# FFN 2's up projection by Strassen's algorithm, F in two groups, and two weight sums by an accumulating DMA

## The chip, the cores and the metric

The kernel runs on 1 core of one Trainium2 chip. The metric is the device time of the whole program in microseconds (us); smaller is better. Times are given for three runs, and a profile shows one further execution with every instruction's start and duration.

## The reference

One layer of a decoder trunk, in float32, for 512 tokens of width 1024. A vector c gives nine modulation vectors (shift, scale and gate for three sub-layers). Around a mixer stand two half-step SwiGLU FFNs:

```python
h = modulate(rms_norm(x, norm_ffn2_g[l]), mod[:, 2, 0], mod[:, 2, 1])
x = x + HALF_STEP * mod[:, 2, 2][:, None, :] * swiglu(h, ffn2_w_in[l], ffn2_w_out[l])
```

where `swiglu(h, w_in, w_out)` splits `h @ w_in` into g and u and gives `(silu(g) * u) @ w_out`. Here h is 512 x 1024, `w_in` 1024 x 5632 (2816 columns of g, 2816 of u) and `w_out` 2816 x 1024. A final RMSNorm over x is the output.

## The kernel before, in words

Activations lie transposed, features over the 128 partitions and the T = 512 tokens along the free axis. D = 1024 is KD = 8 blocks of 128, F = 2816 is KF = 22 blocks. TensorE (PE) multiplies in float32r. Each factor is split into a high part (rounded to float32r) and a rest, and a product is three matmuls into the same PSUM bank: high x high, high weight x rest, rest weight x high (`product`, L1136 to L1138). Each matmul is preceded by a load of its 128 x 128 weight tile.

The stages follow one another: modulation and FFN 1, mixer, the norm ahead of FFN 2, FFN 2 up, FFN 2 down, final norm. In FFN 2's **up projection** one tile is one block of F: `pair` runs 8 blocks of K x 2 (gate and up) x 3 terms = 48 matmuls of 512 columns into two PSUM banks. The first of the 22 tiles is done in halves of 256 tokens, as the norm hands them over. In the **down projection** one block is one of the 8 blocks of D: 22 x 3 = 66 matmuls, in two chunks of 11 x 3. The last block is done in two halves of 256 tokens. In the second FFN, PE also transposes the block before (L1253) for the output.

Each engine runs its own program in order, and semaphores tie them. SyncE (SP) loads raw weights, double-buffered: `load_pair` (L300) 1.05 MB a tile in two DMAs, as soon as the slot's raw weights have been split (`lo_ready`). ScalarE (ACT) casts a slot to its high part (`split_hi`, L497), does silu (L552), and casts the product (L560). VectorE (DVE) subtracts for the rest (`split_lo`, L706), multiplies silu(g) with u (L824), and subtracts for the product's rest (L837). In the down projection DVE adds a block to x (L854), scales it for the output, and adds up squares (L865). GpSimd (POOL) is nearly idle there; it splits three weight slots elsewhere (L429), one of them beside the norm ahead of FFN 2. The norm itself runs in steps of 256 tokens: DVE scales (L752), ACT adds the shift and rounds (`h_his`, L504), DVE takes the rest (L759).

## Time and profile before

| | |
|---|---|
| Three runs | 931.53, 932.56, 933.40 us (median 932.56) |
| Span of the profiled execution, first to last instruction | 929.1 us |
| Median of the runs over that span | 3.5 us |
| PE busy | 885.1 us (95%), 4155 matmuls |
| DVE, ACT, POOL busy | 495.9, 266.4, 60.3 us |
| DMA | 123.64 MB, 133 GB/s over the span |
| Mean granted clock of TensorE | 0.977 of full speed |

The profiled execution's own device time is not listed apart from its span; the runs' median stands 3.5 us over it. A busy share is an average over stages, so what one stage is worth is read from that stage. Matmuls are pipelined, and their durations in the trace overlap the next one, so the distance between two starts is what one costs.

### The profile page before, as it was taken

The page shows a single profiled execution, that of the slowest core. Times are in us where ns is not written, and L with a number is a line of the kernel's source. Part 1 is how long each engine was busy: PE and PEld are TensorE (multiplying, and loading weights), DVE is VectorE, ACT ScalarE, POOL GpSimd, SP SyncE. Part 2 cuts the span into 40 slices and gives each one's busy share as a digit, 9 for nine tenths or more (in the row PEclk, how much of TensorE's full clock was granted, in tenths as well). Part 3 has the DMA queues.
Part 4 walks back from the last instruction along what each step waited for, and adds up shares of the span by engine and source line. Part 5 has one row for each costly group of instructions (what it writes and reads, how often), then busy time and mean ns, then how long its engine had stood idle before and what let it go on. Part 6 is the DMA issues. An engine that isn't in the chain of part 4 may idle for free.

```text
span 929.1 us, 11471 instructions
## 1 busy us (share of the span) xinstructions
PE 885.1 (95%) x4155; PEld 735.3 (79%) x4155; DVE 495.9 (53%) x734; ACT 266.4 (29%) x306; POOL 60.3 (6%) x49
## 2 busy tenths in 40 slices
PE   4499999999999999998999989999999999999997
PEld 3387888888888888896887878888888888888886
DVE  3899877777775656547635574333333333233332
ACT  5123222322222222224324243222223322222222
POOL 2810000000000000002340030000000000000000
PEclk9599999999999999999999999999999999999998
DMA  9929766666646565444332313333333332333322
GB/s 275 294 70 256 203 194 194 198 195 199 183 136 194 153 191 148 130 136 124 83 111 69 91 47 90 92 103 108 104 91 90 90 90 64 91 94 94 93 63 91
DMA packets 205381, 123.64 MB, mean 133 GB/s; under 512 B 4280, under 2 KB 203052, under 8 KB 205356
## 3 DMA queue, kind: packets, MB, share of 16 engines
q1 hardware_dynamic: 205356, 123.28, 46.8%
q8 instruction: 18, 0.29, 0.1%
q14 instruction: 7, 0.06, 0.0%
HBM read 121.17 MB, written 2.10 MB: 133 GB/s over the span
## 4 chain that ended last, share of the span: by engine, by line
PE 91%; DVE 4%; SPq 1%; DMA 1%; issue 1%; ACT 1%; POOL 0%; DVEq 0%
PE ps L1136 29%; PE ps L1138 29%; PE ps L1137 29%; DVE acc_first L962 2%; DVE h_lo L759 1%; PE ps L1378 1%; DMA ada_first<-in_w_ada_dram 1%; PE ps L1379 1%; PE ps L1380 1%; SPq L300 1%; DVE w_lo L717 0%; PE ps L1270 0%; DVE work L752 0%; PE ps L1428 0%; PE ps L1418 0%
## 5 line engine op out<-in xcount | busy, mean ns | idle before, releaser
L1136 PE MATMUL ps<-h_hi,w_hi 128*128 128x512 f32 (+1 forms) x784 | 308.6, 394 | 7.7 <-DVE h_lo L759 6.2
L1138 PE MATMUL ps<-h_hi,w_lo 128*128 128x512 f32 (+1 forms) x784 | 306.3, 391 | 0.0
L1137 PE MATMUL ps<-h_lo,w_hi 128*128 128x512 f32 (+1 forms) x784 | 303.7, 387 | 0.0
L706 DVE TENSOR_TENSOR w_lo<-w_raw,w_hi 128x2048 fp32r<-128x2048 f32 (+1 forms) x81 | 165.2, 2039 | 179.2 <-ACT w_hi L497 179.2
L497 ACT CAST w_hi<-w_raw 128x2048 fp32r<-128x2048 f32 (+1 forms) x83 | 140.7, 1695 | 141.7 <-PE ps L1138 112.4
L1136 PEld LDWEIGHTS ps<-h_hi,w_hi 128*128 128x128 f32 x784 | 149.6, 191 | 37.2 <-DVE h_lo L759 6.8
L1138 PEld LDWEIGHTS ps<-h_hi,w_lo 128*128 128x128 f32 x784 | 149.3, 190 | 32.9
L1137 PEld LDWEIGHTS ps<-h_lo,w_hi 128*128 128x128 f32 x784 | 149.2, 190 | 31.7
L1136 PE MATMUL ps<-a_hi,w_hi 128*128 128x512 f32 (+1 forms) x396 | 146.1, 369 | 0.0
L1138 PE MATMUL ps<-a_hi,w_lo 128*128 128x512 f32 (+1 forms) x396 | 145.6, 368 | 0.0
L1137 PE MATMUL ps<-a_lo,w_hi 128*128 128x512 f32 (+1 forms) x396 | 144.7, 365 | 0.0
L552 ACT ACTIVATE work<-ps 128x512 f32<-128x512 f32 x44 | 26.3, 597 | 327.5 <-PE ps L1138 327.5
L824 DVE TENSOR_TENSOR work<-work,ps 128x512 f32<-128x512 f32 x44 | 30.2, 687 | 161.6 <-ACT work L552 161.5
L802 DVE SCALAR_TENSOR_TENSOR ada_acc<-ada_raw,c_act,ada_acc 128x256 f32<-128x256 f32 x196 | 95.0, 485 | 7.0
L1137 PEld LDWEIGHTS ps<-a_lo,w_hi 128*128 128x128 f32 x396 | 74.4, 188 | 13.0
L1138 PEld LDWEIGHTS ps<-a_hi,w_lo 128*128 128x128 f32 x396 | 74.4, 188 | 12.5
L1136 PEld LDWEIGHTS ps<-a_hi,w_hi 128*128 128x128 f32 x396 | 74.4, 188 | 12.1
L429 POOL TENSOR_TENSOR w_lo<-w_raw,w_hi 128x2048 fp32r<-128x2048 f32 x3 | 13.6, 4540 | 437.3 <-ACT w_hi L520 381.3
L504 ACT ACTIVATE h_hi<-work,mod 128x256 fp32r<-128x256 f32 (+1 forms) x36 | 20.4, 579 | 50.5 <-DVE work L752 50.3
L837 DVE TENSOR_TENSOR a_lo<-work,a_hi 128x512 f32 (+1 forms) x44 | 30.1, 684 | 0.0
L759 DVE SCALAR_TENSOR_TENSOR h_lo<-work,mod,h_hi 128x256 fp32r<-128x256 f32 (+1 forms) x36 | 28.9, 806 | 1.0 <-ACT h_hi L504 0.7
L1136 PE MATMUL ps<-y_hi,w_hi 128*128 128x512 f32 (+1 forms) x80 | 28.2, 352 | 0.0
(124 smaller groups left out, 539.9 us busy)
## 6 DMA issues: line engine op xcount, KB each, us to landing
w_raw<-in_ffn_w_in_dram SPq DMA_DIRECT2D x88, 512.0 KB, 5.1
ada_raw<-in_w_ada_dram SPq DMA_DIRECT2D x56, 512.0 KB, 3.7
w_raw<-in_ffn_w_out_dram SPq DMA_DIRECT2D x32, 384.0 KB, 3.9
w_raw<-in_ffn_w_out_dram SPq DMA_DIRECT2D x32, 320.0 KB, 3.2
ada_first<-in_w_ada_dram SPq DMA_DIRECT2D x16, 512.0 KB, 7.4
w_raw<-in_w_mix_in_dram SPq DMA_DIRECT2D x12, 512.0 KB, 4.7
w_raw<-in_w_mix_out_dram SPq DMA_DIRECT2D x8, 512.0 KB, 4.4
x_tok<-in_x_dram SPq DMA_DIRECT2D x4, 512.0 KB, 5.0
```

The lines of the kernel that those rows point to most:

```text
L497: nc.scalar.copy(w_hi[:, s, 0:n], w_raw[:, s, 0:n]).then_inc(hi_ready, 1)
L504: nc.scalar.activation(h_hi[:, k, cols], work[:, SCALED[i % 4], cols], ACT.Identity, bias=mod_col(3 * n, k)).then_inc(h_hi_ready, 1)
L552: nc.scalar.activation(work[:, 0, :], ps[:, 2 * s, :], ACT.Silu).then_inc(silu_ready, 1)
L706: nc.vector.tensor_tensor(w_lo[:, s, 0:n], w_raw[:, s, 0:n], w_hi[:, s, 0:n].bitcast(F32), ALU.subtract).then_inc(lo_ready, 1)
L759: nc.vector.scalar_tensor_tensor(h_lo[:, k, cols], work[:, SCALED[i % 4], cols], mod_col(3 * n, k), h_hi[:, k, cols].bitcast(F32), ALU.add ...
L802: ins = nc.vector.scalar_tensor_tensor(ada_acc[:], w, c_act[:, k:k + 1], ada_acc[:], ALU.mult, ALU.add)
L824: nc.vector.tensor_tensor(work[:, 1, :], work[:, 0, :], ps[:, 2 * s + 1, :], ALU.mult)\
L837: nc.vector.tensor_tensor(dst, prod, hi.bitcast(F32), ALU.subtract).then_inc(a_ready, 1)
L962: nc.vector.scalar_tensor_tensor(acc, ada_first[:, k, :, q, :], c_act[:, q:q + 1], acc, ALU.mult, ALU.add).then_inc(first_step, 1)
L1136: nc.tensor.matmul(dst, w_h, a_h, start=start, stop=False)
L1137: nc.tensor.matmul(dst, w_h, a_l, start=False, stop=False)
L1138: return nc.tensor.matmul(dst, w_l, a_h, start=False, stop=stop)
```

## The change

Of the 22 tiles of F in FFN 2's up projection, the first two stay as they are (`PLAIN`), and 20 are done by `strassen`. It takes the 2 x 2 form with the weights cut into gate and up (rows of the result) and halves of K, and the activations into halves of K and of T. Seven products, each 4 blocks of K x 3 terms = 12 matmuls of 256 columns, take the place of eight. The four sums of activations are made once (`xs`, `sums_hi`, `sums_lo`). The four sums of weights are made for every tile: two by a DMA that adds one SBUF range to another, issued by POOL, the other two by DVE (`add_blocks`). Some products are started in a PSUM bank, copied out by ACT (`keep_first`, `keep_pair`) and carried on, so the results are put together partly in PSUM and partly by DVE (`sum_pair`, `middle`, `gate_and_up`). Half of a tile's result comes out with its sign turned, which the gate (`-HALF_STEP`) takes up.

The order of the stage changes as well. F is cut into two groups of 11 blocks: up tiles of group 0, the down projection over group 0 for all 8 blocks of D, up tiles of group 1, the down projection over group 1. A down block is now 11 x 3 matmuls, and DVE adds to x twice for each. SP loads a tile in five DMAs of 0.26 MB (1.31 MB). The raw weights have two slots of 3584 columns, the high parts one (`sw_hi`), so a tile's pieces are cast as PE finishes with those of the tile before. The loops of the stage are written out.

The core of the diff (SP, POOL, ACT, DVE, PE in this order; KD = 8, KF = 22, P = 128, KA = 4, TH = 256):

```diff
+    PLAIN = 2
+    GF = KF // 2
+    BL = KD // 2 * P
+    SW = 7 * BL
+    DN = GF * P
+    D1_AT = SW - DN
+    NS = KF - PLAIN
+    N0 = GF - PLAIN
+    PIECES = ((0, 2), (2, 5), (5, 7))
+    def up_item(n):
+        return n + (KD if n >= N0 else 0)
+    def down_item(g, m):
+        return N0 + m + g * (KD + GF)
+    UP_ITEMS = {up_item(n) for n in range(NS)}
+    def pieces(i):
+        return sum(3 if j in UP_ITEMS else 1 for j in range(i))
...
+            def sw_free(i):
+                if i < 2:
+                    sp.wait_ge(lo_ready, UP2 + 1 + i)
+                    sp.wait_ge(chunk_done, UP2 + i)
+                else:
+                    sp.wait_ge(sw_lo_ready, pieces(i - 1))
+            def load_up(n):
+                i, f = up_item(n), PLAIN + n
+                s = i % 2
+                sw_free(i)
+                cols = slice(f * P, (f + 1) * P)
+                to = sw_raw[:, s].rearrange("p (j k n) -> p j k n", k=KA, n=P)
+                for j, h, side in ((1, 0, 1), (6, 1, 1), (0, 0, 0), (4, 1, 0), (2, 0, 1)):
+                    sp.dma_start(to[:, j], w_two[:, h, :, side, cols]).then_inc(sw_full[s], 16)
+            def load_down2(g, m):
+                i = down_item(g, m)
+                s = i % 2
+                sw_free(i)
+                to = sw_raw[:, s, 0:DN].rearrange("p (k n) -> p k n", n=P)
+                for k0, k1 in ((0, GF // 2), (GF // 2, GF)):
+                    sp.dma_start(to[:, k0:k1], w_down[:, g * GF + k0:g * GF + k1, m * P:(m + 1) * P])\
+                      .then_inc(sw_full[s], 16)
...
+            for n in range(NS):
+                i = up_item(n)
+                to = sw_raw[:, i % 2].rearrange("p (j c) -> p j c", c=BL)
+                pool.wait_ge(sw_full[i % 2], landed(i))
+                nc.gpsimd.dma_start(to[:, 1:3], to[:, 0:7:6], accum_op=ALU.add).then_inc(sw_added[i % 2], 16)
...
+            def cast_up(n, c):
+                i = up_item(n)
+                if i == 0:
+                    act.wait_ge(chunk_done, UP2 + 1)
+                elif i - 1 in UP_ITEMS:
+                    act.wait_ge(sw_used, pieces(i - 1) + c + 1)
+                else:
+                    act.wait_ge(sw_used, pieces(i) - 1 if c == 0 else pieces(i))
+                if c == 0:
+                    act.wait_ge(sw_added[i % 2], added(i))
+                else:
+                    act.wait_ge(sw_sum, 2 * n + c)
+                j0, j1 = PIECES[c]
+                nc.scalar.copy(sw_hi[:, j0 * BL:j1 * BL], sw_raw[:, i % 2, j0 * BL:j1 * BL])\
+                    .then_inc(sw_hi_ready, 1)
...
+            def keep_pair(n):
+                act.wait_ge(q_done, 2 * n + 2)
+                if n:
+                    act.wait_ge(pair_sum, n)
+                nc.scalar.copy(pair_keep, ps[:, n % 2 * 2 + 1, :].rearrange("p (a t) -> p a t", a=2))\
+                    .then_inc(q_kept, 1)
...
+            def up_slot(n):
+                if up_item(n) and up_item(n) - 1 in UP_ITEMS:
+                    cast_up(n, 2)
+                    silu_second(n - 1)
+                elif n:
+                    cast_up(n, 1)
+                    cast_up(n, 2)
+                keep_first(n)
+                if n not in (N0 - 1, NS - 1):
+                    cast_up(n + 1, 0)
+                keep_pair(n)
+                if up_item(n) and up_item(n) - 1 in UP_ITEMS:
+                    product_hi(n - 1)
+                if n in (N0 - 1, NS - 1):
+                    cast_down(0 if n < N0 else 1, 0)
+                else:
+                    cast_up(n + 1, 1)
+                silu_first(n)
...
+            def add_blocks(n):
+                i = up_item(n)
+                s = i % 2
+                dve.wait_ge(sw_added[s], added(i))
+                def raw(j):
+                    return sw_raw[:, s, j * BL:(j + 1) * BL]
+                nc.vector.tensor_tensor(raw(3), raw(1), raw(6), ALU.add).then_inc(sw_sum, 1)
+                dve.wait_ge(sw_sum, 2 * n + 1)
+                nc.vector.tensor_tensor(raw(5), raw(3), raw(4), ALU.add).then_inc(sw_sum, 1)
...
+            def rest_up(n, c):
+                i = up_item(n)
+                dve.wait_ge(sw_hi_ready, pieces(i) + c + 1)
+                if i == 0 and c == 2:
+                    dve.wait_ge(chunk_done, UP2 + 2)
+                j0, j1 = PIECES[c]
+                nc.vector.tensor_tensor(lo_piece(c), sw_raw[:, i % 2, j0 * BL:j1 * BL],
+                                        sw_hi[:, j0 * BL:j1 * BL].bitcast(F32), ALU.subtract)\
+                    .then_inc(sw_lo_ready, 1)
...
+            def middle(n):
+                i = up_item(n)
+                dve.wait_ge(sw_used, pieces(i) + 2)
+                if n:
+                    dve.wait_ge(gu_ready, n)
+                nc.vector.tensor_tensor(u2, first_keep, ps[:, n % 2 * 2, TH:T], ALU.subtract)\
+                    .then_inc(u2_ready, 1)
+                dve.wait_ge(u2_ready, n + 1)
+                dve.wait_ge(pair_sum, n + 1)
+                nc.vector.tensor_tensor(gate_up[:, 2], gate_up[:, 2], u2, ALU.add).then_inc(up1_ready, 1)
+            def gate_and_up(n):
+                i = up_item(n)
+                dve.wait_ge(sw_used, pieces(i) + 3)
+                if n:
+                    dve.wait_ge(s_ready, 2 * n)
+                nc.vector.tensor_tensor(
+                    gate_up[:, 0:2], ps[:, n % 2 * 2 + 1, :].rearrange("p (a t) -> p a t", a=2),
+                    ev[:, 3:4].to_broadcast([P, 2, TH]), ALU.add).then_inc(gu_ready, 1)
...
+            def up_slot(n):
+                chained = up_item(n) and up_item(n) - 1 in UP_ITEMS
+                if chained:
+                    gate_and_up(n - 1)
+                if n:
+                    rest_up(n, 1)
+                rest_up(n, 2)
+                if chained:
+                    product_of(n - 1)
+                if n not in (N0 - 1, NS - 1):
+                    add_blocks(n + 1)
+                    rest_up(n + 1, 0)
+                if chained:
+                    product_rest(n - 1)
+                sum_pair(n)
+                middle(n)
+                if n in (N0 - 1, NS - 1):
+                    rest_down(0 if n < N0 else 1, 0)
...
+            for n in range(N0):
+                up_slot(n)
+            for m in range(KD):
+                if m == 0:
+                    gate_and_up(N0 - 1)
+                    product_of(N0 - 1)
+                    product_rest(N0 - 1)
+                if m < KD - 1:
+                    rest_down(0, m + 1)
+                else:
+                    add_blocks(N0)
+                    rest_up(N0, 0)
+                update_part(m)
...
+            def half_product(j, dst, src_hi, src_lo, start, stop):
+                w_h, w_l = sw_block(sw_hi, j), lo_block(j)
+                for k in range(KA):
+                    nc.tensor.matmul(dst, w_h[:, k, :], src_hi[:, k, :], start=start and k == 0, stop=False,
+                                     skip_group_check=True)
+                    nc.tensor.matmul(dst, w_h[:, k, :], src_lo[:, k, :], start=False, stop=False,
+                                     skip_group_check=True)
+                    ins = nc.tensor.matmul(dst, w_l[:, k, :], src_hi[:, k, :], start=False,
+                                           stop=stop and k == KA - 1, skip_group_check=True)
+                return ins
+            def strassen(n):
+                i = up_item(n)
+                a, b = n % 2 * 2, n % 2 * 2 + 1
+                t0, t1 = HALVES
+                if n < 2:
+                    pe.wait_ge(prod_ready, KF + n + 1)
+                else:
+                    pe.wait_ge(s_ready, 2 * n - 3)
+                    pe.wait_ge(gu_ready, n - 1)
+                pe.wait_ge(sw_lo_ready, pieces(i) + 1)
+                half_product(0, ps[:, a, t0], h_hi[:, 0:KA, t0], h_lo[:, 0:KA, t0], True, False)\
+                    .then_inc(q_done, 1)
+                if n == 0:
+                    pe.wait_ge(hsum_lo, 2)
+                half_product(1, ps[:, b, t1], sums_hi[:, 1], sums_lo[:, 1], True, False).then_inc(sw_used, 1)
+                pe.wait_ge(sw_lo_ready, pieces(i) + 2)
+                half_product(2, ps[:, b, t0], sums_hi[:, 0], sums_lo[:, 0], False, False).then_inc(q_done, 1)
+                pe.wait_ge(q_kept, 2 * n + 1)
+                if n == 0:
+                    pe.wait_ge(hsum_lo, 3)
+                half_product(3, ps[:, a, t1], sums_hi[:, 2], sums_lo[:, 2], False, True)
+                half_product(4, ps[:, a, t0], h_hi[:, KA:KD, t0], h_lo[:, KA:KD, t0], False, True)\
+                    .then_inc(sw_used, 1)
+                pe.wait_ge(sw_lo_ready, pieces(i) + 3)
+                pe.wait_ge(q_kept, 2 * n + 2)
+                half_product(5, ps[:, b, t0], h_hi[:, KA:KD, t1], h_lo[:, KA:KD, t1], False, True)
+                if n == 0:
+                    pe.wait_ge(hsum_lo, 4)
+                half_product(6, ps[:, b, t1], sums_hi[:, 3], sums_lo[:, 3], False, True).then_inc(sw_used, 1)
...
+            def down2(g, m, between=None):
+                pe.wait_ge(sw_lo_ready, pieces(down_item(g, m)) + 1)
+                if g == 0 and m >= 2:
+                    pe.wait_ge(x_part, m - 1)
+                elif m < 2 and g == 1:
+                    pe.wait_ge(x_part, KD)
+                elif m >= 2:
+                    pe.wait_ge(x_new, X_AT[2] + m - 1)
+                hi, lo = (v.rearrange("p (k n) -> p k n", n=P) for v in (down_hi(m), down_lo(m)))
+                for k in range(GF):
+                    if m == 0:
+                        b_tile(g, k)
+                    if between:
+                        between(k)
+                    ins = product(ps[:, 4 + m % 2, :], hi[:, k, :], lo[:, k, :], b_hi[:, k, :], b_lo[:, k, :],
+                                  k == 0, k == GF - 1)
+                ins.then_inc(sw_used, 1)
...
```

(`landed`, `added` count semaphore increments; `silu_first`, `silu_second`, `product_of`, `product_hi` and `product_rest` are the silu, the product and its split, as before but with T in halves or 512 columns.)

DVE in the up projection, two tiles as they were: `work` is silu(g) or the product, `ps` PSUM, `w_lo` the rest of the weights.

```order
L824 TENSOR_TENSOR work<-work,ps 128x512 [waits a_ready,silu_ready]
L706 TENSOR_TENSOR w_lo<-w_raw,w_hi 128x1408 [waits hi_ready]
L837 TENSOR_TENSOR a_lo<-work,a_hi 128x512 [waits a_hi_ready]
L824 TENSOR_TENSOR work<-work,ps 128x512 [waits a_ready,silu_ready]
L706 TENSOR_TENSOR w_lo<-w_raw,w_hi 128x1408 [waits hi_ready]
L837 TENSOR_TENSOR a_lo<-work,a_hi 128x512 [waits a_hi_ready]
```

These are the last two tiles, whose weight slot is a down block's (1408 columns); in the loop it is 2048 columns. Three operations a tile.

DVE in one changed tile: `ev` holds the parts of the result, `sw_raw`, `sw_hi`, `sw_lo_a` and `sw_lo_b` the weights.

```order
L1483 TENSOR_TENSOR ev<-ps,ev 128x512 [waits s_ready,sw_used]
L1447 TENSOR_TENSOR sw_lo_a<-sw_raw,sw_hi 128x1536 [waits sw_hi_ready]
L1447 TENSOR_TENSOR sw_lo_b<-sw_raw,sw_hi 128x1024 [waits sw_hi_ready]
L1492 TENSOR_TENSOR work<-ev 128x512 [waits b_ready,up1_ready,s_ready]
L1437 TENSOR_TENSOR sw_raw<-sw_raw 128x512 [waits sw_added1]
L1439 TENSOR_TENSOR sw_raw<-sw_raw 128x512 [waits sw_sum]
L1447 TENSOR_TENSOR sw_lo_a<-sw_raw,sw_hi 128x1024 [waits sw_hi_ready]
L1498 TENSOR_TENSOR b_lo<-work,b_hi 128x512 [waits b_hi_ready]
L1462 TENSOR_TENSOR ev<-ev 128x256 [waits b_prod,q_kept]
L1471 TENSOR_TENSOR ev<-ev,ps 128x256 [waits gu_ready,sw_used]
L1475 TENSOR_TENSOR ev<-ev 128x256 [waits pair_sum,u2_ready]
```

Eleven operations a tile. The first waits for PE's end of the tile before, the fifth for the accumulating DMA.

ACT in one changed tile:

```order
L851 CAST sw_hi<-sw_raw 128x1024 [waits sw_sum,sw_used]
L887 ACTIVATE ev<-ev 128x256 [waits gu_ready]
L870 COPY ev<-ps 128x256 [waits u2_ready,q_done]
L851 CAST sw_hi<-sw_raw 128x1024 [waits sw_added1,sw_used]
L876 COPY ev<-ps 128x512 [waits pair_sum,q_done]
L891 CAST b_hi<-work 128x512 [waits b_prod]
L851 CAST sw_hi<-sw_raw 128x1536 [waits sw_sum,sw_used]
L883 ACTIVATE ev<-ps 128x256 [waits b_prod,u2_ready]
```

Eight operations where there were three. The copy of the PSUM pair (L876), which PE's sixth product waits for, stands behind the cast that waits for the accumulating DMA (`sw_added1`).

## Rows read from the trace of the kernel before

**Rows 1.** The page: busy line and chain by engine, whole program.

```profile
PE 885.1 (95%) x4155; PEld 735.3 (79%) x4155; DVE 495.9 (53%) x734; ACT 266.4 (29%) x306; POOL 60.3 (6%) x49
...
PE 91%; DVE 4%; SPq 1%; DMA 1%; issue 1%; ACT 1%; POOL 0%; DVEq 0%
```

**Rows 2.** Stretch, FFN 2 up: busy per engine, clock, DMA share, GB/s.

```profile
564.69:795.42 230.73, 230.73 (x1011) 189.31 (x1009) 74.54 (x63) 60.51 (x63) 0.00 (x0) 1.00 0.33 91
```

**Rows 3.** PE by time (start, us): first 512-column matmul, first down matmul.

```profile
564.69 0.40 PE L1136 MATMUL ps<-h_hi,w_hi 128*128 128x512 f32 x1
...
795.42 0.39 PE L1136 MATMUL ps<-a_hi,w_hi 128*128 128x512 f32 x1
```

**Rows 4.** The same view: first and last of two runs of 256 columns.

```profile
530.93 0.28 PE L1136 MATMUL ps<-y_hi,w_hi 128*128 128x256 f32 x1
...
536.60 0.28 PE L1138 MATMUL ps<-y_hi,w_lo 128*128 128x256 f32 x1
...
903.90 0.28 PE L1136 MATMUL ps<-a_hi,w_hi 128*128 128x256 f32 x1
...
911.56 0.28 PE L1138 MATMUL ps<-a_hi,w_lo 128*128 128x256 f32 x1
```

**Rows 5.** DVE by form (busy us, mean ns), by tile, by time.

```profile
L706 DVE TENSOR_TENSOR w_lo<-w_raw,w_hi 128x1408 fp32r<-128x1408 f32 x32 | 52.0, 1625 | 111.5 <-ACT w_hi L497 111.5
...
L824 DVE TENSOR_TENSOR work<-work,ps 128x512 f32<-128x512 f32 x44 | 30.2, 687 | 161.6 <-ACT work L552 161.5
...
L860 DVE SCALAR_TENSOR_TENSOR xT<-ps,half_gate,xT 128x256 f32<-128x256 f32 x4 | 1.9, 482 | 9.0 <-PE ps L1138 9.0
...
L717 DVE TENSOR_TENSOR w_lo<-w_raw,w_hi x4: 1216/1482/2405, 28.3 to 73.2; 128x1024 fp32r<-128x1024 f32 x4
...
548.33 0.42 DVE L730 TENSOR_TENSOR work<-ident,small 128x256 f32<-128x256 f32 x1
```

**Rows 6.** ACT groups by form (busy us, mean ns of one).

```profile
L497 ACT CAST w_hi<-w_raw 128x1408 fp32r<-128x1408 f32 x32 | 43.9, 1370 | 112.3 <-PE ps L1138 104.1 <-DMA w_raw<-in_ffn_w_out_dram 8.2
...
L520 ACT CAST w_hi<-w_raw 128x1024 fp32r<-128x1024 f32 x6 | 6.1, 1037 | 0.0
...
L607 ACT COPY out_tok<-ps 128x512 f32 x7 | 4.1, 586 | 25.2 <-PE ps L1253 25.2
...
L593 ACT COPY out_tok<-ps 128x256 f32<-128x256 f32 x2 | 0.7, 372 | 1.4 <-PE ps L1263 1.4
```

**Rows 7.** DVE frees a weight slot; the load, in half us.

```profile
655.30 2.29 DVE L706 TENSOR_TENSOR w_lo<-w_raw,w_hi 128x2048 fp32r<-128x2048 f32 x1 [1.02 <-ACT w_hi L497]
...
658.50:659.00 0.50, 0.50 (x3) 0.38 (x3) 0.00 (x0) 0.00 (x0) 0.00 (x0) 1.00 0.12 37
...
662.50:663.00 0.50, 0.50 (x4) 0.42 (x3) 0.00 (x0) 0.00 (x0) 0.00 (x0) 1.00 0.15 34
```

**Rows 8.** DMA issues (KB, us to landing); SP's issue (ns min/median/max).

```profile
ada_first<-in_w_ada_dram SPq DMA_DIRECT2D x16, 512.0 KB, 7.4
...
out_dram<-out_tok SPq DMA_DIRECT2D x4, 512.0 KB, 3.1
...
L300 SPq DMA_DIRECT2D w_raw<-in_ffn_w_in_dram x88: 372/442/3940, 6.0 to 757.1; - x88
```

**Rows 9.** POOL and DVE by time, norm ahead of FFN 2.

```profile
551.50 4.51 POOL L429 TENSOR_TENSOR w_lo<-w_raw,w_hi 128x2048 fp32r<-128x2048 f32 x1 [10.44 <-ACT w_hi L520]
...
551.87 4.43 DVE L759 SCALAR_TENSOR_TENSOR h_lo<-work,mod,h_hi 128x256 fp32r<-128x256 f32 x1 [0.35 <-ACT h_hi L504]
```

**Rows 10.** Stretch right behind that wait, columns as in rows 2.

```profile
556.35:562.06 5.71, 5.71 (x26) 5.71 (x27) 5.06 (x13) 4.21 (x7) 0.00 (x0) 0.50 0.66 185
```

**Rows 11.** PE and DVE by time, FFN 2's down projection.

```profile
833.64 0.60 PE L1253 MATMUL ps<-ident,work 128*128 128x128 f32 x4
...
836.25 1.63 DVE L706 TENSOR_TENSOR w_lo<-w_raw,w_hi 128x1408 fp32r<-128x1408 f32 x1 [4.72 <-ACT w_hi L497]
```

**Rows 12.** DVE by time: the last of that norm.

```profile
560.15 1.26 DVE L759 SCALAR_TENSOR_TENSOR h_lo<-work,mod,h_hi 128x256 fp32r<-128x256 f32 x3
```

More of the change, by code:

```diff
@@ L90, in build_program, with landed, added @@
     SCALED = (0, 1, 3, 4)
+    HSUM_AT = ((0, HALVES[0]), (0, HALVES[1]), (KD // 2, HALVES[1]), (KD // 2, HALVES[0]))
+    HSUMS = (1, 1 + KD // 2, 1 + KD, 1 + KD + KD // 2)
+    PLAIN = 2
[14 more added lines that the diff above has]
+        return sum(3 if j in UP_ITEMS else 1 for j in range(i))
+    def landed(i):
+        return 16 * sum(5 if j in UP_ITEMS else 2 for j in range(i % 2, i + 1, 2))
+    def added(i):
+        return 16 * sum(1 for j in range(i % 2, i + 1, 2) if j in UP_ITEMS)
     LONG_LAG = {1: KD * KD, 2: KD + 2}
@@ new lines, in _ @@
+            for n in range(N0):
+                up_slot(n)
+            for m in range(KD):
+                if m == 0:
+                    silu_second(N0 - 1)
+                if m < KD - 1:
+                    cast_down(0, m + 1)
+                else:
+                    cast_up(N0, 0)
+                if m == 0:
+                    product_hi(N0 - 1)
+            for n in range(N0, NS):
+                up_slot(n)
+            for m in range(KD - 1):
+                if m == 0:
+                    silu_second(NS - 1)
+                cast_down(1, m + 1)
+                if m == 0:
+                    product_hi(NS - 1)
+                    nc.scalar.activation(dummy, ones[:, 0:1], ACT.Sqrt)
+                square2(m)
+                copy_out(m)
@@ L694, in _ @@
+            act.wait_ge(sq_added, SQ_AT[2] + KD)
             for half in range(2):
@@ new lines, in down2_half @@
+            def down2_half(m, half, between=None):
+                cols = HALVES[half]
+                hi, lo = (v.rearrange("p (k n) -> p k n", n=P) for v in (down_hi(m), down_lo(m)))
+                for k in range(GF):
+                    if between:
+                        between(k)
+                    ins = product(ps[:, LAST_BANK[half], cols], hi[:, k, :], lo[:, k, :], b_hi[:, k, cols],
+                                  b_lo[:, k, cols], k == 0, k == GF - 1)
+                ins.then_inc(last_done, 1)
@@ L1480, in transposes @@
+            for n in range(N0):
+                strassen(n)
+            for m in range(KD):
+                down2(0, m)
+            for n in range(N0, NS):
+                strassen(n)
             def transposes(k):
@@ L1484, in transposes @@
                     sum_last(3, 0, (0,))
-            down(DOWN2, 1, X_AT[2], SQ_AT[2], True, transposes).then_inc(chunk_done, 1)
+            for m in range(KD - 1):
+                down2(1, m, lambda k, m=m: transpose_out(m - 1) if m and k == GF // 2 else None)
+            pe.wait_ge(x_new, X_AT[2] + KD - 2)
+            pe.wait_ge(sw_lo_ready, pieces(down_item(1, KD - 1)) + 1)
+            down2_half(KD - 1, 0)
+            transpose_out(KD - 2)
+            sum_blocks(SQ_AT[2] + KD)
+            down2_half(KD - 1, 1, transposes)
             transpose_half(1)
```

284 lines of the change are left out of this document (250 added, 34 removed).

## The prediction

> **What bounds the kernel now.** I read the page first: PE is busy for 885.1 us of a span of 929.1, and the chain that ended last lies on PE for 91% [rows 1]. So what a change saves on PE counts in full, as long as nothing else becomes late. The change touches FFN 2 alone, so the next view is the stretches. In FFN 2's up projection PE is busy for the whole 230.73 us at the full clock (1.00, the 2.4 GHz level), while DVE works 74.5 us, ACT 60.5 us and the DMA engines a third of the time [rows 2]. In order of time, PE's 512-column matmuls of that stage run from 564.69 to 795.42 us [rows 3]: 21 tiles of F with 48 matmuls each (2 projections, 8 blocks of K, 3 terms of the high/low split), 10.99 us a tile and 228.9 ns from one start to the next. There is no gap; the starts are the price of a matmul here, not its modelled duration.
>
> **The change part by part.** Strassen's scheme takes 7 half-size products for 8. A tile of F becomes 7 products of 4 blocks of K, 3 terms and 256 columns: 84 matmuls of 256 columns for 48 of 512, so 12.5% fewer columns. What a 256-column matmul costs must be read, since a weight load stands before each. The trace has two prices: 51 matmuls from 530.93 to 536.60 us have 113.4 ns a start, 66 from 903.90 to 911.56 have 117.8 ns [rows 4]. The columns alone would make half of 228.9, 114.5. I take 117.8, because it belongs to the down projection of the same FFN and most other short runs look like it, and keep 113.4 for the range. A tile then takes 84 x 117.8 = 9.90 us; 20 of the 22 tiles are changed (2 stay plain): 20 x (10.99 - 9.90) = **21.8 us saved**; by 113.4 it would be 29.3.
>
> The rule that speaks against this: the Trainium skill (TensorE: Matmul & The Clock Gate, LDWEIGHTS) gives a weight load as columns / 1.2 ns, so 107 ns for 128 columns, as long as 256 columns take to stream. If the two didn't overlap, a 256-column matmul would take some 213 ns by that page and the change would lose 140 us; the trace disagrees, with 113.4 to 117.8 ns.
>
> The down projection keeps its matmuls: 8 blocks of 22 x 3 become 16 of 11 x 3. Only block 7 changes: 132 at 117.8 ns become 33 at 228.9 and 66 at 117.8, 0.2 us less.
>
> What must be ready in a tile of 9.90 us. *DVE*, by its order above: splits of 1024, 1536 and 1024 columns, two adds of 512 (the other two weight sums), gate and up, product and its rest at 512, three small ones at 256. With 1.22 us for 1024 (the fastest of four; the slow ones lie where POOL works too), 1.76 for 1536 (1.625 for 1408 plus 128 columns), 0.69 for 512, 0.42 and 0.48 for 256 [rows 5] that is 1.22 + 1.76 + 1.22 + 5 x 0.69 + 2 x 0.42 + 0.48 = 9.0 us. It fits, with 0.9 us to spare, where DVE had some 7 idle us a tile before. *ACT*: casts 1.04 + 1.48 + 1.04, and 512- and 256-column reads at 0.59 and 0.37, two of the first, three of the second [rows 6]: 5.9 us. Order within the tile: DVE's first is the sum for gate and up, which waits for the end of the tile before (0.3 us), so the 1536-column split ends at 0.3 + 0.69 + 1.76 = 2.75 us, and PE's third product wants it after 24 matmuls, at 2.83. That is tight but holds. DVE then reaches the third split's end at 3.97 us.
>
> *The weight loads* are the long loop. The slot for tile n+2 comes free with that third split of tile n, at 3.97 us. Before, a slot freed at 657.59 had its 1.05 MB moved between 658.5 and 662.6 us [rows 7]: 1.1 us to start, 3.9 to move. Now 1.31 MB come in five DMAs (issues of 0.44 us each, 2.2 in all [rows 8], hide under it): 1.1 + 4.9 = 6.0 us, so 9.97 us. Then POOL starts the accumulating DMA of 0.52 MB, and no row shows one. Bounds: below, the 3.1 us of a 0.52 MB store from SBUF; above, the 7.4 us of the slowest 0.52 MB loads [rows 8]. I take 5.0, since it reads two operands and so moves what 1.05 MB move, which took 5.0 [rows 7]. It ends at 15.0 us, which is 5.1 us into tile n+1. There ACT's cast of the first 1024 columns waits for it, and behind that cast ACT's copy of the PSUM pair; 5.1 + 1.04 + 0.59 = 6.7 us, and PE's sixth product wants that copy after 60 matmuls, at 7.07. So it is covered, with 0.3 us to spare: the threshold is about 5.4 us for the accumulating DMA. If it takes longer, every microsecond goes on PE's path in each of some 16 tiles (20 less the first two of each group, whose slots were loaded ahead).
>
> The Trainium skill (DMA: Bandwidth & Descriptors, Anatomy of one DMA) fits a GpSimd-issued DMA as 2.0 us plus bytes / 436e3: 3.2 us for 0.52 MB, 4.4 for twice that. By it the loop is covered too; no row here shows such a DMA.
>
> *Entering the stage.* DVE ends the norm at 561.4 us [rows 12], and the plain pair of matmuls on PE runs from 564.69 for 10.99 us. Until then DVE has the four sums over T and K (1024 columns plus 12 x 0.48), four rests of 1024, one product, its rest, two adds and two splits: some 1.2 + 5.8 + 4.9 + 1.4 + 1.4 + 3.0 = 17.7 us, and a wait of about 1 us for the first silu, which PE lets start at 564.69 [rows 3]. It is done about 580, where PE would start tile 0 at 575.7 and wants ACT's copy for its fourth product at 579.9. That copy stands behind the second plain tile's product, so PE waits about 1.7 us, once. *Changing stages.* Each down group's first weight block is cast only behind PE's fifth product (7.07 + 0.3, 1.37 cast, 1.63 rest), 10.4 us against 9.9: 0.5 us, twice. Back to the up projection, DVE's update of block 7 stands ahead of the 1536-column split: 0.7 us, once. *Second down group:* blocks of 33 x 0.229 + 0.68 = 8.24 us; from its transposes to the end of the next rest took 4.24 us before (833.64 to 837.88 [rows 11]) and they now start at 3.43 us of a block, so the rest is there at 7.7. Covered by 0.5 us.
>
> Sum: -21.8 - 0.2 + 1.7 + 1.0 + 0.7 = **-18.6 us**. The span of 929.1 us lies 3.5 us under the runs' median of 932.56, taken as the same after: 932.6 - 18.6 = **914.0 us**.
>
> **The rivals.**
> - *The loop of loads is late* (slower if it is enough). Mechanism: the accumulating DMA ends after 5.4 us, ACT's cast waits, the PSUM copy behind it waits, PE waits at the sixth product in each of 16 tiles. Price: 16 us per microsecond; at 7.4 us it is 32 us more, 946 us. It eats the 18.6 us at 1.2 us over the threshold, so from 6.6 us on the kernel is slower. For it: nothing in the trace shows such a DMA, and the margin is 0.3 us. Against: it moves no more than a load that took 5.0. Half of its chance is over 5.4 and under 6.6 (914 to 932 us), half above.
> - *POOL and DVE hold each other up.* POOL's 4.51 us operation at 551.50 made a 256-column DVE operation last 4.43 us instead of 0.48 [rows 9], and the 4.2 us in which PE was idle brought its clock to 0.50, the 1.2 GHz level, for the next 26 matmuls [rows 10]. If POOL's making of descriptors blocks DVE for 2 us in each tile, DVE's 9.0 becomes 11.0 and a tile 11.0 to 11.2: the gain is gone, about 935 us, and more where the clock falls. Against: POOL does no arithmetic here in that stage. The Trainium skill (SBUF — State Buffer, on the shared port pair) says whoever starts first holds the pair for the whole instruction, and that descriptors wait for DVE's two-port operations; rows 9 agree with the first half, none show the second.
> - *The short matmuls run at 113.4 ns:* 7.5 us more saved, 906.5 us. For it: rows 4's first run. Then the 1536-column split (2.75 against 2.72 us) starts to cost a little.
> - *It doesn't do what it says:* by the instruction order each changed tile does have 84 matmuls of 256 columns. I give this no chance.
>
> **How the numbers follow.** Forecast (within 905 to 920): 0.45. Matmuls at 113.4: 0.12. Late loop below 6.6 us: 0.15, still faster. Late loop above: 0.16, slower. POOL against DVE: 0.09, mostly slower. The rest 0.03. That gives faster 0.73, within 0.2% (1.9 us, about what a measurement of this kernel can tell from no change) 0.03, slower 0.24. The range reaches from 904 (113.4 ns, some waits) to 938, which takes in most of the late loop and leaves out its far end. The likeliest case's own range is 905 to 920.
>
> **What would show each step.** Right: 84 starts in about 9.9 us, no idle time of PE before its third, fourth and sixth product in most tiles, POOL's DMA landing in some 5 us, an add on DVE that rarely waits for it. Wrong: idle time of PE released by ACT's copy into the PSUM keep tile, itself released by a DMA on POOL's queue (late loop); DVE operations far over 1.2 us for 1024 columns (the port); a granted clock under 1.00 in the stage. The forecast falls if a tile takes over 11 us.

## The result, and the profile after

The changed kernel takes 940.87 us (median of 4 runs, 935.48 to 946.08) against 932.04 before in the same comparison: ratio 1.0103, 95% interval 1.0055 to 1.0150. In a second comparison it took 938.59 us against 931.70: ratio 1.0073 (1.0036 to 1.0110). It is slower by some 7 to 9 us where 18.6 less were forecast. The profile below is of the slowest of the first four executions (946.08 us).

The page of the changed kernel, first the busy line and the chain by engine, then the DMA issues (KB each, median us from issue to landing):

```profile
PE 878.7 (93%) x4842; PEld 760.3 (81%) x4842; DVE 607.4 (64%) x920; ACT 323.8 (34%) x410; POOL 84.4 (9%) x69
...
PE 73%; DMA 10%; DVE 8%; SPq 4%; issue 2%; ACT 2%; POOL 1%; ACTq 0%; DVEq 0%
...
sw_raw<-in_ffn_w_in_dram SPq DMA_DIRECT2D x100, 256.0 KB, 4.4
...
sw_raw<-sw_raw POOLq DMA_DIRECT2D x20, 512.0 KB, 5.5
```

PE has less to do than in [rows 1] (878.7 against 885.1 us) and the span is longer, 944.4 us. PE's share of the chain fell from 91% to 73%, and DMA's rose from 1% to 10%. The accumulating DMA, of which no row of before told, takes 5.5 us.

The stretches of the changed up tiles, 9 in the first group and 11 in the second (busy us and count of PE, PEld, DVE, ACT, POOL, then granted clock, DMA share, GB/s):

```profile
581.18:690.45 109.27, 96.14 (x757) 95.03 (x755) 75.51 (x99) 50.33 (x73) 8.40 (x7) 0.94 0.57 134
...
751.03:871.28 120.25, 112.35 (x925) 110.73 (x923) 89.69 (x118) 60.83 (x86) 10.80 (x9) 0.99 0.67 154
```

Before, the stage was all PE [rows 2]. Now a tile takes 12.1 us in the first group and 10.9 in the second, not 9.90, and PE is busy for 96.1 of 109.3 and 112.4 of 120.3 us. The 20 tiles take 229.5 us where 20 plain ones took 219.7.

Who waited for whom in the changed kernel (us in total, times, longest us):

```profile
ACT sw_hi L851 <- DMA sw_raw<-sw_raw: 76.9, 16, 9.8
...
DVE sw_raw L1437 <- DMA sw_raw<-sw_raw: 35.9, 14, 5.8
...
PE ps L1929 <- ACT ev L876: 18.4, 11, 4.6
```

That is one chain: the DMA is late, ACT's cast waits for it (76.9 us), and PE waits 18.4 us for L876, the copy of the PSUM pair that stands behind this cast. In the second changed tile the wait was longest (4.86 us from start to start), and the clock fell behind it. The stretch of that wait and the one behind it:

```profile
599.80:604.60 4.80, 0.27 (x3) 0.07 (x1) 1.65 (x3) 1.62 (x3) 0.00 (x0) 0.96 1.12 248
...
604.65:610.50 5.85, 5.85 (x38) 5.85 (x39) 3.90 (x7) 3.50 (x5) 1.20 (x1) 0.74 0.59 111
```

In the 5.85 us behind the wait the clock is 0.74 on average, so PE was at the 1.2 GHz level for part of it, as in [rows 10]. Counted over the 1680 starts of the changed tiles, 15 gaps of over 0.3 us hold 24.8 us, 23.0 more than 15 normal steps of 0.118, and steps of 0.19 to 0.3 us, most of them at the lower clock, cost 7.7 us more than at 0.118. Together that is 31 of the 31.5 us that the tiles lost against 20 x 9.90 = 198.

So the 15.3 us between the spans (944.4 and 929.1) come from three places (by PE's starts at the stages' ends): +9.8 in the changed tiles, +0.3 in the rest of FFN 2, and +5.5 ahead of it, in code that the change leaves alone. The last is FFN 1's up projection; first a stretch of it before, then the same in the changed kernel:

```profile
120.00:160.00 40.00, 40.00 (x176) 32.84 (x175) 30.96 (x50) 9.31 (x11) 0.00 (x0) 1.00 0.62 182
```

```profile
120.00:160.00 40.00, 40.00 (x173) 32.41 (x172) 29.46 (x47) 10.45 (x11) 0.00 (x0) 1.00 0.65 184
```

173 matmuls in 40 us instead of 176, without any wait. This needed an experiment of its own.

### The profile page after: what moved, and what is told of

The parts are those of the page before. It is cut to its first block, busy times and chain, and to the rows that moved or that the text cites. A ratio compares the mean times of both kernels' runs of the same rounds, so it can differ in the third digit from the quotient of the medians.

```text
span 944.4 us, 12863 instructions
## 1 busy us (share of the span) xinstructions
PE 878.7 (93%) x4842; PEld 760.3 (81%) x4842; DVE 607.4 (64%) x920; ACT 323.8 (34%) x410; POOL 84.4 (9%) x69
## 4 chain that ended last, share of the span: by engine, by line
PE 73%; DMA 10%; DVE 8%; SPq 4%; issue 2%; ACT 2%; POOL 1%; ACTq 0%; DVEq 0%
PE ps L1580 21%; PE ps L1581 20%; PE ps L1582 20%; DMA sw_raw<-sw_raw 5%; DMA sw_raw<-in_ffn_w_in_dram 4%; PE ps L1929 2%; PE ps L1933 2%; PE ps L1931 2%; SPq L515 2%; DVE acc_first L1218 1%; DVE h_lo L1017 1%; DVE sw_lo_b L1447 1%; SPq L391 1%; PE ps L1822 1%; PE ps L1823 1%
## 5 line engine op out<-in xcount | busy, mean ns | idle before, releaser
L1580 PE MATMUL ps<-h_hi,w_split 128*128 128x512 f32 (+1 forms) x464 | 183.6, 396 | 7.3 <-DVE h_lo L1017 5.7
L1581 PE MATMUL ps<-h_lo,w_split 128*128 128x512 f32 (+1 forms) x464 | 182.2, 393 | 0.0
L1582 PE MATMUL ps<-h_hi,w_split 128*128 128x512 f32 (+1 forms) x464 | 181.9, 392 | 0.0
L964 DVE TENSOR_TENSOR w_split<-w_raw,w_split 128x2048 fp32r<-128x2048 f32 (+1 forms) x45 | 93.3, 2072 | 87.3 <-ACT w_split L627 87.3
L627 ACT CAST w_split<-w_raw 128x2048 fp32r<-128x2048 f32 (+1 forms) x47 | 81.0, 1723 | 99.5 <-PE ps L1582 73.7
L1580 PEld LDWEIGHTS ps<-h_hi,w_split 128*128 128x128 f32 x464 | 89.0, 192 | 27.6 <-DVE h_lo L1017 6.6
L851 ACT CAST sw_hi<-sw_raw 128x1024 fp32r<-128x1024 f32 (+1 forms) x60 | 71.4, 1194 | 110.5 <-DMA sw_raw<-sw_raw 76.9
L1582 PEld LDWEIGHTS ps<-h_hi,w_split 128*128 128x128 f32 x464 | 89.0, 192 | 19.2
L1581 PEld LDWEIGHTS ps<-h_lo,w_split 128*128 128x128 f32 x464 | 89.0, 192 | 18.5
L1929 PE MATMUL ps<-sums_hi,sw_hi 128*128 128x256 f32 x320 | 90.8, 284 | 2.0 <-ACT ev L870 1.5
L1931 PE MATMUL ps<-sums_lo,sw_hi 128*128 128x256 f32 x320 | 90.8, 284 | 0.0
L1929 PE MATMUL ps<-h_hi,sw_hi 128*128 128x256 f32 x240 | 70.1, 292 | 18.4 <-ACT ev L876 18.4
L1580 PE MATMUL ps<-a_hi,w_split 128*128 128x512 f32 (+1 forms) x198 | 73.3, 370 | 0.0
L1581 PE MATMUL ps<-a_lo,w_split 128*128 128x512 f32 (+1 forms) x198 | 73.0, 369 | 0.0
L1582 PE MATMUL ps<-a_hi,w_split 128*128 128x512 f32 (+1 forms) x198 | 72.2, 364 | 0.0
```

The lines of the kernel that those rows point to most:

```text
L627: nc.scalar.copy(w_hi[s][:, 0:n], w_raw[s][:, 0:n]).then_inc(hi_ready, 1)
L851: nc.scalar.copy(sw_hi[:, j0 * BL:j1 * BL], sw_raw[:, i % 2, j0 * BL:j1 * BL])\
L964: nc.vector.tensor_tensor(w_lo[s][:, 0:n], w_raw[s][:, 0:n], w_hi[s][:, 0:n].bitcast(F32), ALU.subtract).then_inc(lo_ready, 1)
L1580: nc.tensor.matmul(dst, w_h, a_h, start=start, stop=False)
L1581: nc.tensor.matmul(dst, w_h, a_l, start=False, stop=False)
L1582: return nc.tensor.matmul(dst, w_l, a_h, start=False, stop=stop)
```

## The experiments

Two theories were set against each other. **Late loop**: the way from the freeing of a weight slot over load and accumulating DMA is longer than a ring of two slots, used in turn, allows. **Full engines**: DVE with its 9.0 us a tile, or a hold-up between DVE and POOL as in [rows 9], is the bound. Every ratio is to the kernel before in the same comparison, with its 95% interval.

**The changed kernel again, as a control.** No edit.

> The changed kernel once more, unaltered, as the control of this call. Its first profile lost time in two places: FFN 1's up projection, whose code is unchanged, ran at 173 matmuls per 40 us instead of 176 to 177 (about 6 us more), and the changed up tiles took 12.1 us each in the first group and 10.9 us in the second, instead of 9.9. Theory 'late loop': 936 to 946 us again, and PE idle ahead of its sixth product, released by ACT's copy of the PSUM pair. Rival 'one odd execution' (the first profile is the slowest of four runs): 918 to 930 us.

Measured: 938.59 us (933.41 to 942.38, 6 runs). This profile is of a 933.41 us execution, the fastest of the six, and FFN 1 is at 176 matmuls per 40 us in it. One turn of the loop in it follows. DVE by time (the third split of a tile ends within 0.1 us of where L1492 begins; L1437 is the first add on the sums):

```profile
798.35 0.68 DVE L1492 TENSOR_TENSOR work<-ev 128x512 f32<-128x512 f32 x1
...
809.24 0.68 DVE L1492 TENSOR_TENSOR work<-ev 128x512 f32<-128x512 f32 x1
...
811.85 0.69 DVE L1437 TENSOR_TENSOR sw_raw<-sw_raw 128x512 f32<-128x512 f32 x1 [1.92 <-DMA sw_raw<-sw_raw]
```

POOL's accumulating DMA, ACT's cast and copy behind it, and PE's fifth and sixth product:

```profile
806.35 1.20 POOL L616 DMA_DIRECT2D sw_raw<-sw_raw  x1 [9.75 <-DMA sw_raw<-in_ffn_w_in_dram]
```

```profile
811.90 1.05 ACT L851 CAST sw_hi<-sw_raw 128x1024 fp32r<-128x1024 f32 x1 [4.28 <-DMA sw_raw<-sw_raw]
...
812.85 0.58 ACT L876 COPY ev<-ps 128x512 f32<-128x512 f32 x1
```

```profile
812.58 0.28 PE L1933 MATMUL ps<-h_hi,sw_lo_a 128*128 128x256 f32 x1
...
813.58 0.36 PE L1929 MATMUL ps<-h_hi,sw_hi 128*128 128x256 f32 x1 [0.71 <-ACT ev L876]
```

The slot is free at 798.44 us, POOL starts its DMA at 806.35, the sums are there at 811.85: 7.9 and 5.5 us, 13.4 for a way that I had at 11.0. ACT's cast starts at 811.90, its copy ends at 813.43, and PE starts its sixth product at 813.58, 1.00 us after the last start of the fifth. The stretches of this execution, first the two groups of changed tiles and then parts of that turn, show where the load's extra time goes:

```profile
575.73:678.96 103.23, 91.95 (x757) 90.50 (x756) 75.68 (x99) 50.35 (x73) 8.40 (x7) 0.98 0.60 141
739.52:858.62 119.10, 111.27 (x926) 109.32 (x924) 89.67 (x118) 60.63 (x86) 10.80 (x9) 1.00 0.68 156
...
799.50:800.00 0.50, 0.50 (x6) 0.50 (x6) 0.00 (x0) 0.00 (x0) 0.00 (x0) 1.00 1.46 164
800.00:800.50 0.50, 0.50 (x6) 0.50 (x5) 0.00 (x0) 0.00 (x0) 0.00 (x0) 1.00 0.50 95
800.50:801.00 0.50, 0.50 (x7) 0.50 (x6) 0.00 (x1) 0.00 (x0) 0.00 (x0) 1.00 1.13 337
...
802.00:802.50 0.50, 0.00 (x0) 0.00 (x0) 0.50 (x2) 0.50 (x3) 0.00 (x0) 1.00 0.64 152
...
803.50:804.50 1.00, 1.00 (x11) 1.00 (x10) 1.00 (x4) 0.99 (x1) 0.00 (x0) 1.00 1.11 322
...
805.50:806.50 1.00, 1.00 (x11) 1.00 (x10) 0.67 (x2) 0.67 (x1) 0.15 (x1) 1.00 0.01 2
...
808.50:809.00 0.50, 0.50 (x7) 0.50 (x6) 0.50 (x1) 0.00 (x0) 0.00 (x0) 1.00 1.08 188
```

Until 800.2 us the bytes that move are those of the previous accumulating DMA (164 GB/s; it moves 188 alone at 808.5 too), and the load's first byte comes only then, 1.8 us after the slot is free; the load runs at up to 340 GB/s with a dip to 152 at 802. Its last packet starts at 805.6, 5.4 us after the first, and POOL starts 0.7 us later. I had left this last step, from the last byte to the next engine, out of my 6.0. The two groups took 103.2 and 119.1 us, 11.5 and 10.8 a tile, so here the changed tiles lose 2.6 us against the plain ones and 24.3 against 198; the loss of 7 to 9 us in the medians lies between this profile and the first.

**The weight buffers' places alone.** In the kernel before:

```diff
-        w_raw = sb("w_raw", [P, 2, FULL])
-        w_hi = sb("w_hi", [P, 2, FULL], F32R)
-        w_lo = sb("w_lo", [P, 2, FULL], F32R)
...
         ada_T = sb("ada_T", [P, UNIT])
+        w_raw = sb("w_raw", [P, 2, FULL])
+        w_split = sb("w_split", [P, 2, 2, FULL], F32R)
+        w_hi, w_lo = w_split[:, :, 0], w_split[:, :, 1]
```

> The kernel before with one thing of the change: its weight buffers lie in SBUF where the changed kernel has them (modulation buffers first, then raw weights, then high and low parts side by side per slot); all instructions as before. Theory 'placement': if where the weights lie sets the start-to-start time of the 512-column matmuls, FFN 1's up projection runs at 173 matmuls per 40 us and the kernel takes 936 to 939 us. Rival 'run to run': 930 to 934 us, 176 to 177 matmuls per 40 us.

Measured: 931.84 us, ratio 1.0006 (0.9986 to 1.0026). FFN 1 in it:

```profile
120.00:160.00 40.00, 40.00 (x176) 32.82 (x175) 31.02 (x50) 9.26 (x11) 0.00 (x0) 1.00 0.64 182
```

176 matmuls with the new places, and 176 in the control, which is the changed kernel itself: the places do not bring the slow loop about. The profile of the next experiment has 173 to 174 again, those of all later ones 176 or 177, with the same FFN 1. The two slow ones are the slowest executions of their kernels, so it is a property of an execution, worth 5.5 us in the first profile, and no part of the change's price. What sets it stays open.

**No accumulating DMA.** POOL's DMA is left out, and ACT and DVE wait for the load:

```diff
-                nc.gpsimd.dma_start(to[:, 1:3], to[:, 0:7:6], accum_op=ALU.add).then_inc(sw_added[i % 2], 16)
...
-                    act.wait_ge(sw_added[i % 2], added(i))
+                    act.wait_ge(sw_full[i % 2], landed(i))
...
-                dve.wait_ge(sw_added[s], added(i))
+                dve.wait_ge(sw_full[s], landed(i))
```

> The changed kernel without POOL's accumulating DMA: ACT and DVE wait for the raw weights' load instead. Left out: two of the four weight sums, so the output is another. Theory 'late loop' (the accumulating DMA's some 6.5 us from the load's landing to its own set the tile): the changed tiles fall to 9.9 us and the kernel takes 913 to 922 us. Rival 'DVE and ACT are too full': tiles stay over 10.5 us and the time over 930 us. Rival 'the late matmuls': a price of 118 ns a start holds in both.

Measured: 912.45 us, ratio 0.9785 (0.9753 to 0.9817). The two stretches of changed tiles:

```profile
580.04:671.31 91.27, 89.48 (x757) 89.06 (x756) 75.17 (x99) 50.97 (x73) 0.00 (x0) 1.00 0.41 118
...
731.88:841.98 110.10, 109.26 (x926) 108.85 (x924) 88.89 (x118) 61.56 (x86) 0.00 (x0) 1.00 0.42 122
```

91.3 us for 9 tiles and 110.1 for 11, at a clock of 1.00 and with DVE and ACT as busy as before. DVE and ACT are not too full; the loop is the loss. (POOL's work is gone here as well; the staged loads below keep it.) The start-to-start time is 117.9 ns over 720 and over 900 matmuls. This run also shows the load without an accumulating DMA beside it. A slot comes free at 785.85 us, where this split ends:

```profile
784.63 1.22 DVE L1446 TENSOR_TENSOR sw_lo_b<-sw_raw,sw_hi 128x1024 fp32r<-128x1024 f32 x1
```

```profile
786.50:787.00 0.50, 0.50 (x7) 0.50 (x6) 0.50 (x1) 0.40 (x1) 0.00 (x0) 1.00 0.04 12
```

The first byte comes 1.05 us later, as in all 20 turns of this run (1.03 to 1.09). In the control it came 1.1 to 2.9 us after the slot was free in the twelve turns in which the previous accumulating DMA still moved bytes, each time within 1.1 us of that DMA's last byte. So the accumulating DMA lengthened the way twice: by its own 5.5 us, and by holding up the next load.

**ACT's copy ahead of its cast.**

```diff
-                if n not in (N0 - 1, NS - 1):
-                    cast_up(n + 1, 0)
                 keep_pair(n)
+                if n not in (N0 - 1, NS - 1):
+                    cast_up(n + 1, 0)
```

> The changed kernel with two of ACT's operations exchanged: the copy of the PSUM pair stands ahead of the cast of the next tile's first 1024 columns, which waits for the accumulating DMA. Nothing is left out. Theory 'late loop through ACT's order': the copy is done at about 5.2 us of a tile, PE no longer waits at the sixth product, and DVE's chain bears a landing up to about 5.9 us into the tile; 918 to 928 us. Rival 'the DMA is simply too late for the next tile too': PE then waits at the next tile's start or third product instead, and the time stays at 933 to 943 us.

Measured: 936.93 us, ratio 1.0041 (1.0020 to 1.0062). My theory missed here, the rival held:

```profile
ACT sw_hi L851 <- DMA sw_raw<-sw_raw: 47.2, 15, 9.3
...
PE ps L1929 <- DVE sw_lo_a L1447: 17.3, 18, 2.5
```

PE no longer waits for the copy, but 17.3 us for the splits of weight pieces (L1447), about half each at a tile's first and third product. DVE does these later since its add waits for the same DMA. To move a wait from one product to another does nothing while the loop sets the pace.

**Staged loads.** SP loads each block as soon as its own piece of the slot has been split:

```diff
+                staged = i >= 2 and i - 2 in UP_ITEMS
+                if not staged:
+                    sw_free(i)
...
-                for j, h, side in ((1, 0, 1), (6, 1, 1), (0, 0, 0), (4, 1, 0), (2, 0, 1)):
+                for j, h, side in ((1, 0, 1), (0, 0, 0), (2, 0, 1), (4, 1, 0), (6, 1, 1)):
+                    if staged and j in (1, 2, 6):
+                        sp.wait_ge(sw_lo_ready, pieces(i - 2) + {1: 1, 2: 2, 6: 3}[j])
```

> The changed kernel with SP's loads of a tile staged: each of the five blocks is loaded as soon as its own piece of the slot has been split (blocks 0 and 1 behind the first split, 2 and 4 behind the second, 6 behind the third) and no longer all five behind the third. Nothing is left out. In the control's trace the way from the third split's end to the landing of the sums was 13.4 us (7.9 for 1.31 MB, 5.5 for the accumulating DMA) for a tile of 10.8. Theory 'late loop': now only 0.26 MB stand behind the third split, some 3.5 + 5.5 = 9 us, less than a tile; PE no longer waits at the sixth product; 912 to 922 us. Rival 'the accumulating DMA itself fights with the loads': its 5.5 us grow as loads now lie beside it, and the time stays over 930 us.

Measured: 913.62 us, ratio 0.9800 (0.9775 to 0.9824), with the accumulating DMA at 5.6 us. DVE and POOL by time, and the second group's stretch:

```profile
781.91 1.22 DVE L1451 TENSOR_TENSOR sw_lo_b<-sw_raw,sw_hi 128x1024 fp32r<-128x1024 f32 x1
...
783.05 0.68 DVE L1496 TENSOR_TENSOR work<-ev 128x512 f32<-128x512 f32 x1
...
793.54 0.69 DVE L1441 TENSOR_TENSOR sw_raw<-sw_raw 128x512 f32<-128x512 f32 x1
```

```profile
787.65 1.20 POOL L620 DMA_DIRECT2D sw_raw<-sw_raw  x1 [9.29 <-DMA sw_raw<-in_ffn_w_in_dram]
```

```profile
728.60:839.26 110.66, 109.50 (x926) 108.91 (x924) 89.08 (x118) 60.87 (x86) 10.80 (x9) 1.00 0.70 168
```

The slot's last piece is free at 783.13 us, POOL starts at 787.65 and DVE adds at 793.54 without a wait: 4.5 + 5.6 = 10.1 us for the way that was 13.4. The DMA engines are even busier (0.70 of the time against 0.68) and a tile takes 10.06 us. So bandwidth was not the trouble, and the same accumulating DMA is in time once the loads ahead of it are shorter: it was the sum of the way that was too long, and shortening either end of it helped. POOL still issues 20 of these DMAs here, so a hold-up between POOL and DVE is ruled out as well.

**Staged loads and the copy ahead of the cast.** Both edits.

> Both edits: staged loads, and ACT's copy of the PSUM pair ahead of the cast that waits for the accumulating DMA. Nothing is left out. Theory 'late loop': the same as staged loads alone within 3 us, 912 to 920 us, since the order on ACT matters only while the DMA is late. Rival: a further gain of over 5 us, which would say that the DMA is still late in some tiles.

Measured: 912.58 us, ratio 0.9797 (0.9775 to 0.9819); and as a control in a later comparison:

> The kernel of e5 once more, as the control of this call: 911 to 914 us. It also shows whether the second group's start-to-start time of 116.7 ns (117.9 in the first group) comes back: if it is the kernel's, 116.7 again; if it is one execution's, 117.9.

Measured: 914.09 us, ratio 0.9802 (0.9788 to 0.9817), with 117.9 ns a start in both groups where the first execution had 116.7 in the second. As expected the order on ACT is worth nothing measurable once the DMA is in time.

**All sums on DVE**, no accumulating DMA, the copy ahead of the cast:

```diff
+                to = sw_raw[:, s].rearrange("p (j c) -> p j c", c=BL)
+                nc.vector.tensor_tensor(to[:, 1:3], to[:, 1:3], to[:, 0:7:6], ALU.add).then_inc(sw_added[s], 16)
```

> All four weight sums on DVE, one addition of 1024 columns more a tile (1.22 us), no accumulating DMA, and ACT's copy of the PSUM pair ahead of the cast. Nothing is left out. DVE has 10.2 us of work for a tile of 9.9. Theory 'late loop is all of the loss': the loop is 5.5 us shorter, tiles take 10.1 to 10.5 us, the kernel 916 to 926 us. Rival 'DVE's chain, not the DMA': tiles over 11 us, the kernel at 935 us or more.

Measured: 914.66 us, ratio 0.9811 (0.9789 to 0.9833), a little better than I gave it. In the second group:

```profile
733.76:839.27 105.51, 105.10 (x901) 104.91 (x901) 98.56 (x126) 59.95 (x83) 0.00 (x0) 1.00 0.44 127
```

DVE is busy for 98.6 of 105.5 us and PE for 105.1. I had its work at 10.2 us a tile and left out that one operation often starts some 0.08 us before the end of the one ahead of it, with twelve operations a tile. The two sums could as well have stayed on DVE.

**An accumulating DMA of one block.**

```diff
-                nc.gpsimd.dma_start(to[:, 1:3], to[:, 0:7:6], accum_op=ALU.add)
+                nc.gpsimd.dma_start(to[:, 1:2], to[:, 0:1], accum_op=ALU.add)
```

> The changed kernel with an accumulating DMA of one block instead of two (0.26 MB instead of 0.52). Left out: one of the four weight sums, so the output is another. Theory 'the DMA is mostly a fixed price': issue to landing falls from 5.5 to some 4.3 us, a gain of 1 us a tile, some 10 us in all. Rival 'price by bytes': it falls to about 3 us.

Measured: 918.95 us (one run, so there is no interval). The DMA, KB each and us to landing:

```profile
sw_raw<-sw_raw POOLq DMA_DIRECT2D x20, 256.0 KB, 3.3
```

3.3 us for 0.26 MB and 5.5 for 0.52: the rival held, the price goes by bytes. A line through the two sizes gives 2.2 us for each 0.26 MB and 1.1 us fixed, an estimate from two points. The kernel is some 20 us faster than the control, where I had expected 10: with 2.2 us less on the way the tiles of the second group no longer wait (900 starts at 117.7 ns on end). The first group still waits 3.0 us in its second changed tile.

**The opening.** Both edits of before, and in the first changed tile `keep_first(0)` ahead of `plain_silu(1)` on ACT:

```diff
+            keep_first(0)
             plain_silu(1)
...
-                keep_first(n)
+                if n:
+                    keep_first(n)
```

> Staged loads and the copy ahead of the cast, as before in e5, and one more exchange on ACT: in the first changed tile the copy of the first product (keep_first) stands ahead of the second plain tile's silu, cast and the wait for DVE between them. Nothing is left out. PE's idle 1.77 us ahead of the first tile's fourth product was released by that copy. Theory 'it was only queued behind the plain tile': the gap goes, 1 to 1.7 us less than e5. Rival 'the third rest of the sums over T and K is as late' (DVE's, which the same product waits for): the gap shrinks by under 0.5 us and the time stays.

Measured: 911.38 us, ratio 0.9790 (0.9772 to 0.9807), against 914.09 of the same kernel without this edit in the same comparison. PE ahead of the fourth product in the control, and what is left with the edit, ahead of the sixth:

```profile
581.62 0.38 PE L1929 MATMUL ps<-sums_hi,sw_hi 128*128 128x256 f32 x1 [1.48 <-ACT ev L870]
```

```profile
583.33 0.39 PE L1935 MATMUL ps<-h_hi,sw_hi 128*128 128x256 f32 x1 [0.24 <-DVE sw_lo_b L1453]
```

The 1.48 us of idle time are gone, 0.24 are left. But a new wait stands in the third changed tile:

```profile
599.81 0.39 PE L1935 MATMUL ps<-sums_hi,sw_hi 128*128 128x256 f32 x1 [0.46 <-DVE sw_lo_a L1453]
```

By PE's starts the edit is worth some 0.5 us net in this profile. The rest of what separates the two profiles is mostly the step of 116.6 ns in long runs of this one against 117.9 in its control. The 2.7 us between the medians therefore can't be put down to the edit: the executions overlap (910.60 to 914.57 and 912.87 to 915.72 us). This version has the lowest median that was run, 2.1% under the kernel before, but is not shown to be faster than the other versions with the loop in time.

## Why the prediction was wrong, point by point

- **The bound and the stage**: right. The stage was PE alone, and with the loop in time the change gives what was forecast: 911 to 915 us in the four versions that have the loop in time and leave nothing out, 914.0 forecast.
- **84 x 117.8 ns = 9.90 us a tile**: right, 117.9 measured over 1620 matmuls.
- **The weight load against 256 columns** (the Trainium skill, TensorE: Matmul & The Clock Gate, LDWEIGHTS): the trace's word held, load and matmul overlap at 256 columns for 100 us on end.
- **DVE 9.0 and ACT 5.9 us a tile**: they fit, as forecast, and both sums were a little high; in the changed kernel DVE did 165.2 us in 20 tiles, 8.3 each, and ACT 111.2, 5.6 each. The sums left out that operations overlap by some 0.08 us. A split of 1024 columns took 1219 ns, as forecast:

```profile
L1447 DVE TENSOR_TENSOR sw_lo_b<-sw_raw,sw_hi 128x1024 fp32r<-128x1024 f32 x20 | 24.4, 1219 | 0.0
```

- **POOL against DVE** (rival, 0.09): did not happen. POOL is busy 1.2 us for each accumulating DMA, and DVE's operations kept their durations. The rule of the Trainium skill (SBUF — State Buffer, Who interferes with whom) on descriptors that wait concerns DVE operations in a 2-port mode, and it gives tensor_tensor none; DVE's eleven operations a tile are all TENSOR_TENSOR. The trace agrees as far as it goes: no split became longer.
- **The long loop: the step that failed.** "1.1 + 4.9 = 6.0 us" for the load was 7.9: 1.8 to the first byte, since the previous accumulating DMA was still moving (1.05 without one), 5.4 to move, which was 5.3 to 6.2 without an accumulating DMA too and so simply sized too low, and 0.7 from the last byte to POOL's start, which the sum put at nothing. "I take 5.0" for the accumulating DMA was 5.5. The margin of 0.3 us carried none of that. The rival with 0.31 is what came: the way was 2.4 us too long, PE waited at the sixth product behind ACT's cast, as it said.
- **The price of lateness: half right.** I wrote 16 us per microsecond. In a ring of two slots the same way is run once in two tiles. Let P be the tile and L the way: the sums come 3.97 + L - P into the next tile, cast and copy take 1.75 with the hand-overs, and 24 matmuls (2.83 us) follow, so P = 3.97 + L - P + 4.58, P = (L + 8.55) / 2. With L = 13.4 that is 10.98 us; 10.8 to 10.9 were measured in the second group. With the one-block DMA, L = 13.4 - 2.2 = 11.2, it is 9.9, and no tile of the second group waited. A microsecond of L over 11.25 costs half a microsecond a tile. What made the loss larger was the first group: its second changed tile waited 4.6 us in the control too, because the opening frees the first slot late (at 583.15 us, 7.4 into the first tile, not 3.97) and the way was 14.1 us there (sums at 597.2); that wait also lowered the clock. I had set the loop aside for the first two tiles of each group. By my price the 2.1 us over the margin would have cost 34 us; the changed tiles lost 31.5 in the first profile and 24.3 in the control. That these are near is luck: two errors of opposite sign.
- **The Trainium skill's fit for such a DMA** (DMA: Bandwidth & Descriptors, Anatomy of one DMA), 3.2 us for 0.52 MB or 4.4 for twice that: both under the 5.5 measured; the measurement decides.
- **Opening 1.7, back to up 0.7, down groups covered**: right (1.65 and 0.70 over the normal step in the profiles with a loop in time, no waits between the down blocks). Into the down groups PE's first start came 0.58 us behind the last of the up tiles, 0.46 over a normal step, for the 0.5 forecast.
- **5.5 us of FFN 1** in the first profile: not the change's, and no step of the sum.
